# Delta-rule turns: the last small level turned in one piece, ScalarE setting the diagonal blocks, and the three engines' orders dealt anew

## The reference, cut

```python
def gated_deltanet(u, w_in, conv_w, a_log, dt_bias, norm_gain, w_out):
    proj = u @ w_in
    qkv = jax.nn.silu(causal_dwconv(proj[..., :GDN_QKV_DIM], conv_w))
    z = proj[..., GDN_QKV_DIM:GDN_QKV_DIM + GDN_VAL_DIM].reshape(B, S, GDN_V_HEADS, GDN_HEAD_V)
...
    q = jnp.repeat(l2_norm(q) * (GDN_HEAD_K ** -0.5), rep, axis=2)
    k = jnp.repeat(l2_norm(k), rep, axis=2)
...
    o = chunk_gated_delta_rule(q, k, v, g, beta)
    o = rms_norm(o, norm_gain) * jax.nn.silu(z)
    return o.reshape(B, S, GDN_VAL_DIM) @ w_out

def chunk_gated_delta_rule(q, k, v, g, beta):
...
    m = jnp.where(strict, beta[..., :, None] * kk * decay, 0.0)
    a = m + jnp.eye(C, dtype=f32)
    rhs = jnp.concatenate([v * beta[..., None], k * (beta * jnp.exp(gc))[..., None]], axis=-1)
    sol = lax.linalg.triangular_solve(a, rhs, left_side=True, lower=True, unit_diagonal=True)
...
```

## Time and profile before

| | us |
|---|---|
| median of 3 runs (1778.39, 1782.19, 1781.95) | 1781.95 |
| the profiled execution | 1779.81 |
| its span, first to last instruction | 1778.0 |
| PE busy (matmul) in the span | 1734.3 (98%) |
| DVE busy | 1419.0 (80%) |
| ACT busy | 1011.8 (57%) |

### The profile page before, as it was taken

One profiled execution on the slowest core, in us unless ns is written; L12 is line 12 of the kernel. 1 busy time (PEld: TensorE's weight loads), 2 busy tenths in 40 slices (PEclk: granted clock), 3 DMA queues, 4 the chain that ended last, 5 costly groups with the idle time before them and its releaser, 6 DMA issues.

```text
span 1778.0 us, 32327 instructions
## 1 busy us (share of the span) xinstructions
PE 1734.3 (98%) x12926; PEld 1547.9 (87%) x12926; DVE 1419.0 (80%) x2433; ACT 1011.8 (57%) x1680; POOL 85.3 (5%) x163
## 2 busy tenths in 40 slices
PE   7999999999999999999999999999999999999998
PEld 6888888888888898889888888888898889988887
DVE  4758889788877588888988877898989898867664
ACT  3657764666765577655655322655556555566553
POOL 0000001000000000000001100010101010000000
PEclk9999999999999999999999999999999999999999
DMA  5256559443332356568788833788978787536552
GB/s 197 88 186 201 190 187 347 143 144 131 112 117 85 120 202 212 189 238 313 280 284 293 322 133 105 281 309 283 322 252 315 275 319 266 164 130 205 189 190 95
DMA packets 102819, 373.90 MB, mean 210 GB/s; under 512 B 11440, under 2 KB 11600, under 8 KB 102544
## 3 DMA queue, kind: packets, MB, share of 16 engines
q1 hardware_dynamic: 80352, 289.77, 46.5%
q0 software_dynamic: 22320, 82.09, 13.6%
HBM read 370.74 MB, written 1.08 MB: 209 GB/s over the span
## 4 chain that ended last, share of the span: by engine, by line
PE 83%; DVE 8%; ACT 4%; issue 2%; DMA 2%; DVEq 0%; SPq 0%; ACTq 0%
PE ps L650 36%; PE ps L653 20%; PE ps L657 2%; DVE weights_lo L618 2%; PE ps L658 2%; PE ps L659 2%; PE ps L1074 2%; PE ps L748 2%; PE ps L1259 1%; PE ps L2369 1%; ACT weights_hi L611 1%; DMA ffn_tiles<-in_ada 1%; DVE arena L2488 1%; PE ps L2395 1%; DVE u L2045 1%
## 5 line engine op out<-in xcount | busy, mean ns | idle before, releaser
L618 DVE TENSOR_TENSOR weights_lo<-weight_ring,weights_hi 128x1024 fp32r<-128x1024 f32 x493 | 601.5, 1222 | 129.4 <-ACT weights_hi L611 128.9
L611 ACT ACTIVATE weights_hi<-weight_ring 128x1024 fp32r<-128x1024 f32 x493 | 518.1, 1057 | 159.5 <-PE ps L650 104.8
L650 PE MATMUL ps<-u_halves,weights_hi 128*128 128x512 f32 x2048 | 495.0, 391 | 0.9 <-DVE u_halves L473 0.5
L650 PEld LDWEIGHTS ps<-u_halves,weights_hi 128*128 128x128 f32 x2048 | 376.3, 188 | 75.8 <-DVE weights_lo L618 1.0
L653 PEld LDWEIGHTS ps<-u_halves,weights_lo 128*128 128x128 f32 x2048 | 266.0, 191 | 10.4 <-DVE weights_lo L618 0.3
L653 PE MATMUL ps<-u_halves,weights_lo 128*128 128x256 f32 x2048 | 274.2, 283 | 0.2
L650 PE MATMUL ps<-act_halves,weights_hi 128*128 128x512 f32 x952 | 231.6, 391 | 0.1
L650 PEld LDWEIGHTS ps<-act_halves,weights_hi 128*128 128x128 f32 x952 | 173.4, 188 | 33.0 <-DVE weights_lo L618 0.5
L887 DVE SCALAR_TENSOR_TENSOR ffn_tiles<-ffn_tiles,cond 128x1024 f32<-128x1024 f32 x144 | 175.3, 1219 | 5.3 <-DMA ffn_tiles<-in_ada 5.1
L780 ACT ACTIVATE ffn_tiles<-ps 128x512 f32<-128x512 f32 x128 | 76.0, 594 | 143.9 <-PE ps L653 143.7
L657 PE MATMUL ps<-u_halves,weights_hi 128*128 128x256 f32 x456 | 137.8, 302 | 16.0 <-DVE u L2045 12.7
(11 more groups left out here) (346 smaller groups left out, 2342.9 us busy)
## 6 DMA issues: line engine op xcount, KB each, us to landing
weight_ring<-in_w SPq DMA_DIRECT2D x545, 512.0 KB, 3.9
ffn_tiles<-in_ada POOLq DMA_DIRECT2D x144, 512.0 KB, 5.4
scaled<-gates_scratch POOLq DMA_DIRECT2D x8, 512.0 KB, 5.4
arena<-in_alibi POOLq DMA_DIRECT2D x1, 1536.0 KB, 6.8
h<-in_x SPq DMA_DIRECT2D x4, 256.0 KB, 3.6
out<-u SPq DMA_DIRECT2D x4, 256.0 KB, 2.1
consts<-in_consts SPq DMA_DIRECT2D x1, 592.0 KB, 9.5
cond<-in_cond SPq DMA_DIRECT2D x1, 512.0 KB, 10.3
```

The source lines that it names most:

```text
L611: nc.scalar.activation(w_slot(s)[0], ring[:, n % RING], ACT.Copy).then_inc(hi_ready, 1)
L618: nc.vector.tensor_tensor(lo, ring[:, n % RING], hi.bitcast(F32), ALU.subtract).then_inc(lo_ready, 1)
L650: return nc.tensor.matmul(ps[:, bank], hi, halves, start=start, stop=stop, skip_group_check=True)
```

## The change

At level 3, ACT first copies the whole product into `x_`, as at the smaller levels, and tells DVE at once (`g_x32`); then it makes the three quarter copies that level 4 reads (`x64`). DVE turns `x_` in one transpose for each chunk into `xb`. A new function `diagonal_act` on ACT copies the four turned quarters from `xb` into the diagonal of `xt_`, and PE's second step of level 4 waits for it (`g_diag`). Beside that the calls of all three engines stand in another order within a turn; on PE only half of unit 9 moves.

```diff
@@ level_second_pe
-                if 0 < lv <= SMALL:
+                if 0 < lv < SMALL:
                     pe.wait_ge(g_xb, blocks_until(i, lv - 1, t))
+                if lv == SMALL:
+                    pe.wait_ge(g_diag, 2 * i + t + 1)
...
                     if lv == SMALL:
-                        pe.wait_ge(g_xb, blocks_until(i, lv - 1, 1))
+                        pe.wait_ge(g_x, 2 * (LEVELS - 1) * i + 2 * SMALL)
@@ gdn_turn_pe
             first_values_pe(pe, i)
+            gdn_unit_pe(pe, n, 9, (0,))
             v_turn_pe(pe, n)
             cross_pe(pe, i)
             kk_pe(pe, n)
-            gdn_unit_pe(pe, n, 9)
+            gdn_unit_pe(pe, n, 9, (1,))
             second_values_pe(pe, i)
@@ level_chunk_act
                 elif lv == SMALL - 1:
-                    for r in QUARTERS[0], HALVES[1]:
+                    nc.scalar.activation(flat(x_[:, t]), ps[:, bank, 0:GB * Q], ACT.Copy).then_inc(g_x32, 1)
+                    if i == 0 and t == 0:
+                        act.wait_ge(g_cleared, 2)
+                    for r in QUARTERS[0], QUARTERS[2]:
                         nc.scalar.activation(x64[r, t, :, 0:Q], heads(r, bank), ACT.Copy)
                     r = QUARTERS[1]
                     last = nc.scalar.activation(x64[r, t, :, Q:H], heads(r, bank), ACT.Copy)
...
+        def diagonal_act(act, i, t):
+
+            act.wait_ge(g_xb, blocks_until(i, SMALL - 1, t))
+            for r in QUARTERS:
+                last = nc.scalar.activation(xt_[r, i % 2, t, :, r], xb[r, t], ACT.Copy)
+            last.then_inc(g_diag, 1)
@@ gdn_last_turn_act
             level_act(act, i, 3)
+            diagonal_act(act, i, 0)
+            diagonal_act(act, i, 1)
             split_hi(act, "gdn_out", 6)
@@ turn_blocks_dve
-                dve.wait_ge(g_x, 2 * (LEVELS - 1) * i + 2 * lv + t + 1)
                 if lv < SMALL - 1:
-                    last = nc.vector.transpose(flat(xb[:, t]), flat(x_[:, t]))
+                    dve.wait_ge(g_x, 2 * (LEVELS - 1) * i + 2 * lv + t + 1)
                 else:
-                    for n, r in enumerate(QUARTERS):
-                        at = Q if n == 1 else 0
-                        last = nc.vector.transpose(xt_[r, i % 2, t, :, r], x64[r, t, :, at:at + Q])
+                    dve.wait_ge(g_x32, 2 * i + t + 1)
+                last = nc.vector.transpose(flat(xb[:, t]), flat(x_[:, t]))
                 last.then_inc(g_xb, 1)
@@ gdn_turn_dve
+            level_dve(dve, i, 3)
+            gdn_lo_dve(dve, n, 3)
+            taps_conv_dve(dve, steps, n, 4)
+            turn_blocks_dve(dve, i, 3)
+
+            level_dve(dve, i, 4)
+            taps_conv_dve(dve, steps, n, 5)
+            gdn_lo_dve(dve, n, 4)
+            m_table_dve(dve, steps, n)
+            gdn_lo_dve(dve, n, 5)
+
+            level_dve(dve, i, 5)
+            taps_conv_dve(dve, steps, n, 6)
+            gdn_lo_dve(dve, n, 6)
+            taps_conv_dve(dve, steps, n, 7)
+            qk_norm_dve(dve, steps, n)
+            gdn_lo_dve(dve, n, 7)
+
+            rest_dve(dve, i)
+            gdn_lo_dve(dve, n, 8)
...
+            out_gate_dve(dve, i)
             gdn_lo_dve(dve, n, 9)
             gdn_lo_dve(dve, n, 10)
-            out_gate_dve(dve, i)
-            gdn_lo_dve(dve, n, 11)
```

More of the change, by code:

```diff
@@ L1361, in build @@
             "g_level_product", "g_level_masked", "g_x_product", "g_xt_product", "g_x_copied", "g_xt_copied"))
+        g_x32, g_diag = sem("g_last_small_x_copied"), sem("g_block_diagonal")
         g_v0, g_v0c, g_c, g_r1, g_v1, g_v1c = (sem(n) for n in (
@@ L1825, in level_chunk_act @@
         def level_chunk_act(act, i, lv, t):
-            if i == 0 and lv == SMALL - 1 and t == 0:
-                act.wait_ge(g_cleared, 2)
             heads = lambda r, bank, n=Q: ps[r, bank, 0:GB * n].rearrange("p (n s) -> p n s", n=GB)
@@ L2223, in gdn_dve @@
             masked_products_dve(dve, steps, 0)
-            for j in (9, 10, 11):
+            for j in (9, 10):
                 gdn_lo_dve(dve, 0, j)
@@ L2266, in gdn_turn_dve @@
             taps_conv_dve(dve, steps, n, 6)
+            gdn_lo_dve(dve, n, 6)
             taps_conv_dve(dve, steps, n, 7)
             qk_norm_dve(dve, steps, n)
-            gdn_lo_dve(dve, n, 6)
-            m_table_dve(dve, steps, n)
+            gdn_lo_dve(dve, n, 7)
             rest_dve(dve, i)
-            gdn_lo_dve(dve, n, 7)
+            gdn_lo_dve(dve, n, 8)
+            if i == 1:
+                mix_lo_dve(dve, 0)
             unit_lower_dve(dve, n, 0)
@@ L2288, in gdn_last_turn_dve @@
             turn_blocks_dve(dve, i, 0)
+            gdn_lo_dve(dve, i, 11)
             level_dve(dve, i, 1)
```

60 lines of the change are left out of this document (27 added, 33 removed).

## The result

The kernel after takes **1758.49 us** in the median (four runs, 1756.32 to 1760.05) against 1782.07 (four runs, 1778.39 to 1784.72): ratio 0.9868, 95% interval 0.9846 to 0.9891, so 1.3% faster. The forecast was 1765.0, with 1761.5 as the low end; the change gave more than that. Run again beside the first experiments it took 1760.04 (four runs) against 1783.42 (eleven): 0.9872, 0.9856 to 0.9888. The profiled execution took 1760.05 us, 19.76 less than that of before; 18.56 of these lie in the four turns, the last one up to its first values.

What follows compares the result with a forecast made beforehand. PE bounds the turns and loses time in waits set by queue order. Waits of 9.8 + 0.7 + 2.2 plus 3.35 us half clock make 16.05, less 1 for handovers: 1779.8 - 15.05 = 1764.8, forecast 1765, own range 1761.5 to 1768.5, taken to 1774.

Steps and rivals of the forecast that it cites:

- The bound: Delta-rule turns: PE bounds a turn, busy 58.50 of 62.15 us in turn 1; DVE and ACT have 8 us or more spare.
- the place of the waits: PE waits 9.8 us on convolution taps, longest after level 4's first matmuls ahead of unit 6, short ones before units 2, 4.
- the walk from level 4 on: Timing count from level 4's first matmuls: diagonal copies 0.6 us to spare, unit 6's taps 0.5 us or more before unit 8.
- the waits on the taps: PE's eight waits of projection units on DVE's convolution taps, 9.8 us, all claimed to go.
- the new end of the turn on VectorE: Late splits 9, 10 move behind the output gate; turn 0's level 0 masked product has one split less ahead: 0.7 us.
- half clock 3.35: Turn 2's PE work lost 3.35 us to a half-clock stretch behind a gap; claimed to go with that gap.
- last turn, level 4: Low half of the mix comes 1.9 us earlier, level 4's second half begins near 588.3, not 590.6: 2.2 us, half clock included.
- The allowance: 1 us taken off the summed gain for handovers the walk leaves out, 0.03 to 0.1 us each, 0.4 in turn 1.
- The rival that the clock is not given back: Only the waits go; 3.35 and 1.2 us of half clock stay: 1769.3 us, chance 0.13.
- The renamed waits: PE waits on DVE's splits instead of its taps: 1780 us, chance 0.06.
- the slower rival: DVE falls behind at the rest product; at 10 us of lag 1786.7 us, chance 0.06.
- the late ScalarE: ScalarE, with 2.7 us more a turn, becomes the late engine, 2.4 us a turn: 1773 us, chance 0.13.

Runs made afterwards that it cites:

- the first experiments: One-piece transposes alone, the order alone, after again and the gap put back, run beside the kernel before at 1783.42 us.
- unit 9 whole: Kernel after with unit 9 of the projections whole at its old place on TensorE, behind kk: 1764.78 us, ratio 0.9889.
- one-piece transposes alone: Kernel before with the one-piece transposes, extra PSUM copy and eight diagonal copies on ScalarE, old queue orders kept: 1767.08 us, ratio 0.9904.
- the order alone: Kernel after with the eight quarter transposes of before and no diagonal copies, all new orders kept: 1762.88 us, ratio 0.9887.

## Why the prediction fell short, and where it held

**What held.** The bound (PE, by its waits), the place of the waits, and the walk from level 4 on. It had 0.6 us for the diagonal copies and 0.5 to 1.1 us at unit 8; the trace shows 0.5 and 0.6. The copies were taken at 268 ns with 395 as the far end; they take 306 (turn 0's groups; busy us, mean ns):

```profile
L1863 ACT ACTIVATE arena<-arena 32x128 f32<-32x128 f32 x8 | 2.4, 306 | 0.1
```

The estimate of 200 ns from the Trainium skill ("ScalarE: Activation LUTs", "What ACT_TABLE_LOAD costs") doesn't hold here: four copies in 1.27 us are 0.32 each, with no overlap to be seen, and the measurement decides. Other copies of the same turn do overlap: eight of 128x128 (L1821) have 397 ns each and take 2.18 us together. The turns came out at 58.41, 58.04 and 59.05 us, against 58.5 to 59. That the waits on the taps would all go, and that nothing else would take their place, was right, and so was the new end of the turn on VectorE, put at 0.7 us in turn 0 and nothing elsewhere (0.76 by the trace). That nothing waits at the transposes of v was luck in part: the prediction put half of unit 9 at no cost and no gain, and without it each turn waits there for about 1 us.

**What failed is the sum.** The prediction entered each wait with the idle time that the list gives, and then took 1 us off for handovers, 15.05 in all; 19.76 is what the two profiles differ by. Of the 6.5 us by which the median lies below the forecast 4.7 are that difference, 1.6 come from two of the four runs that lie below the profiled one (run again, the median was 1760.04), and the rest is rounding. The mechanism was right; the sizes of the terms were off, and two stood at nothing. The terms, each against what it measured:

| | forecast | measured |
|---|---|---|
| turn 0 (2.36 + 0.53 + 0.71) | 3.60 | 4.05 |
| turn 1 (0.87 + 0.53 + 2.23) | 3.63 | 4.11 |
| turn 2 (0.87 + 0.53 + 1.85, half clock 3.35) | 6.60 | 7.26, less 1.06 for a new hole |
| last turn, level 4 | 2.2 | 2.76 |
| last turn, old holes and rest | 0 | 1.29 + 0.15 |
| outside the turns (0.8 of it a gap at 1070 us) | 0 | 1.2 |
| handovers | -1.0 | 0 |
| sum (15.05 with the rounded rows) | 15.03 | 19.76 |

*Three terms of stalls, 1.6 us.* Behind a unit's matmuls a stall costs more than its idle time. The rows of after show why the figure is low: matmuls start 0.12 us apart (458.73, 458.85) and are drawn 0.28 us long, so the time between a drawn end and the next start leaves 0.16 us out. In the experiments one stall of 0.99 us cost 1.18 (unit 9 whole, turn 0), one of 1.23 cost 1.35; 2.05 us in four waits (turn 1 of the one-piece transposes alone) cost 2.76. Behind level 4's small matmuls it cost hardly more than shown (1.03 for 1.03, 2.35 for 2.29).

*The allowance, 1.0 us, should have been nothing.* It was meant for handovers that would become waits; there are none, since each lies under PE's work.

*The last turn, 0.56.* The prediction let level 4's second matmuls begin when all four parts of the masked product are done (+3.57 us from level 4's start); they begin at +2.77 with the first two. Part of that is given back, as the second half then waits.

*Holes and the rest, 1.6, entered at nothing.* Most of it lies outside the turns: a wait at 1070 us has 1.23 us before and 0.41 after, and 1.22 again in the kernel with the order alone, so it is luck. PE's holes without a named wait move from build to build: 0.70 and 0.14 us at level 1 of the last turn before, one of 0.90 in turn 2 after, at the same matmul in both of its profiles (504.36, 504.20). They cost 1.29 and 1.06. What they are stays open.

**The clock was weighed by one profile.** "The 2.1 us by which the median lies above the profiled run, not carried over", was an assumption about the median after, and that part was right; but a profile of before was one draw. The 37 runs of before beside the experiments have a median of 1783.39 and mean clocks of 0.988 to 0.995; the profiled one had 0.995, as high as the highest of them. The nine runs at 0.991 average 1785.97, the twelve at 0.993 1781.74. After's eight have 0.997 to 1.000 and a median of 1759.98. So before ran more often at half the clock than its profile showed, and the medians of these runs differ by 23.4 us, 3.6 more than the profiles. By a least-squares line through the 37 (1.5 us for 0.001) the clock's share of the 23.4 is 6 x 1.5 = 9 us, from 0.992 to 0.998 in the medians, an estimate beyond the line's own end; the prediction had 3.35 and some 1.2 in the last turn.

The rival that the clock is not given back is out: no turn of after has a stretch below 1.00, nor has one of the two parts alone. The renamed waits and the slower rival are out by the list of PE's waits, and so is the late ScalarE, for whose copies that list has no wait.

## What to carry to other kernels

When a wait disappears because its engine's queue has been put in order, ask what else would have removed it: here shorter transposes and earlier taps each took most of the same gaps, and the sum of their single gains is more than half as large again as the gain of both. Enter a stall of TensorE with the start-to-start time, not with the idle time of the list, and take nothing off for handovers that lie under its work. Where gaps and half clock go together, read the granted clock of all runs before using one profile's as the cost.
